# Convolved feed-forward, up projection: pairing high and low x in one 512-column matmul

## The chip, the cores and the metric

The kernel runs on one core of a Trainium2 chip. The metric is the device time of one execution in microseconds (us), the median of several runs. The engines are TensorE (PE; its weight loads are listed as PEld), VectorE (DVE), ScalarE (ACT), GpSimd (POOL) and SyncE (SP), which issues the weight stream's DMAs. Each engine works through its own list of instructions in order and waits only on semaphores.

## The reference

Two two-layer transformer blocks over 256 positions of width 1024, in float32. The part that is changed is the feed-forward of the second block, in both of its layers:

```python
h = rms_norm(x, norm_ffn_g[l])
u = causal_depthwise_conv(h @ ffn_w_up[l], ffn_conv_w[l], ffn_conv_b[l])   # 1024 -> 2 x 2816, 3 taps
x = x + (silu(u[..., :D_FF]) * u[..., D_FF:]) @ ffn_w_down[l]              # 2816 -> 1024
```

## The kernel before

**Numbers in two parts.** Every float32 operand of a product is split into a high part (rounded to fp32r) and a low part (the rest): a = ah + al. A product is three matmuls that add up in one PSUM bank: high weights with high x, high weights with low x, low weights with high x.

**The weight stream.** All weights come as units of 128 x 2048 numbers, in the order of use, through four slots (`raw`, `whi`, `wlo`). For unit U, SP loads `raw`; ScalarE makes the high part, `hi(U)` (L592), once the unit has landed and TensorE has used unit U - 4; VectorE makes the low part, `lo(U)` (L1143), and counts `lo_ready`, which frees `raw` for the next load and `whi`, `wlo` for TensorE. TensorE counts `unit_used`.

**The up product.** The 5632 columns are cut into CTF = 11 blocks, j = 0 to 10, of 512 columns: four groups f of 128, two of the gate half and two of the up half. A block takes two units, U1 + 2j and U1 + 2j + 1 (half the depth each). Block 0 is made with x as the stationary operand and turned; blocks 1 and 2 have the weights stationary and the x that isn't yet divided by its root mean square (`scaled_u` multiplies the result by the row `krow`); from j = RAW_X = 3 on the matmuls read `xs`, x already scaled: four rows of 1024, high m=0, low m=0, low m=1, high m=1, so that `xs_h` is rows 0 and 3 and `xs_l` rows 1 and 2. In `up_straight(j)` each group f and depth tile kt has three matmuls of 256 columns (L2518, L2520, L2521), 96 in a block. A block fills two PSUM banks; the eight banks (`acc` four, `tb` four) hold four blocks in turn (`up_bank`). The wait for block j is for the taps of block j - 4:

```python
elif j >= 4:
    pe.wait_ge(f_t2, CTF * l + j - 3)
```

**The convolution and gate.** For block j ScalarE makes `tap2(j)` (L1050, four instructions, tap 2 and the bias) from PSUM into `cv`; VectorE adds the other two taps, `taps10(j)` (L1710, eight instructions, from PSUM), and counts `f_t2`; ScalarE applies Silu, `fsilu(j)` (L1056); VectorE multiplies, `product(j)` (L1717, into `pr`); ScalarE makes the high part `fhi(j)` (L1063, into `yth`), VectorE the low part `flo(j)` (L1743, into `ytl`). Blocks 6 and 8 (`FSEVEN_POS`) go into a down product of seven instead of eight block products ("seven"); for it VectorE makes three sums, `y_sums` (L1727 to L1732), ScalarE their high part (L1067), VectorE their low part, `y_sums_lo` (L1738). In `fhi` ScalarE waits for these sums, and its copy for them follows.

**The order around it** is written out by hand. In the loop over j = 4 to 11 ScalarE has `hi(U1+2j+2)`, `tap2(j-1)`, `hi(U1+2j+3)`, `fsilu(j-2)`, `fhi(j-2)`, and VectorE `lo(U1+2j+2)`, `taps10(j-1)`, `lo(U1+2j+3)`, `product(j-2)`, `flo(j-2)`. The semaphores `f_t0`, `f_si`, `f_pr`, `f_hi` tie each step to the one of the other engine that it needs.

**The down product** (`out_product`) then takes 11 units with matmuls of 512 columns (L1850 to L1852), 24 for a plain unit. The sevens need the weights' sums (`sums`, L1153 to L1158, behind a `lo` of 1536 columns, L1141; ScalarE's `sums_hi`, L597; VectorE's `sums_lo`, L1163, into `fwsum_l`) before their fourth product.

Of the kernel before, what the change touches and what calls it, by code (L numbers as in the profile page):

```python
# [84 lines left out]
def two_blocks_kernel(nc, x_in, stream, cols, bs_col, ws_t, gs_row, fin_row, fin2_row, rel_rows, ffn_cw,  # L85
                      conv_w, conv_ln, moba_g, gla_g, gate_w, gate_b, gate_in, out):
    ctx = ExitStack()
    with ctx:
# [89 lines left out]
        fsum = at("fsum", [2 * 3 * P], o_sc)  # L178
        fsum_l = at("fsum_l", [2 * 3 * P], o_sc, F32R)
        fsum_h = at("fsum_h", [2 * 3 * P], o_sc + 2 * 3 * P, F32R)  # L180
        fwsum_at = (o_xh, o_sc + 5120)
        fwsum = [at(f"fwsum{i}", [2048], o) for i, o in enumerate(fwsum_at)]
        fwsum_l = [at(f"fwsum_l{i}", [2048], o, F32R) for i, o in enumerate(fwsum_at)]
        fwsum_h = [at(f"fwsum_h{i}", [2048], o + 2048, F32R) for i, o in enumerate(fwsum_at)]
# [51 lines left out]
        acc = [ctx.enter_context(nc.psum_tensor(f"acc{i}", [P, 512], F32)) for i in range(4)]  # L236
# [4 lines left out]
        def score_parts(b0, i):  # L241
# [17 lines left out]
        n_add, n_tr, n_gm, n_hi, n_lo, n_sq, n_ms, n_r = (  # L259
            sem("norm_" + n) for n in ("added", "transposed", "gained", "hi", "lo", "squared", "meaned", "rms"))  # L260
# [3 lines left out]
        side_made, x_r2 = sem("side_made"), sem("mix_own_rms")  # L264
        a_ev, a_vsq, a_vsum, a_ms, a_r, a_vn, a_sp, a_spc, a_y, y_banks, a_hi, a_lo = (
            sem("gmlp_" + n) for n in ("act", "v_squared", "v_summed", "v_meaned", "v_rms", "v_normed", "spatial",
# [12 lines left out]
        f_ev, f_tr, f_t0, f_t1, f_t2, f_si, f_pr, f_hi, f_lo = (  # L279
            sem("ffn_" + n) for n in ("kept", "transposed", "tap2", "tap1", "tap0", "silu", "product", "hi", "lo"))  # L280
# [3 lines left out]
        x_ltr, x_bn, x_ag, x_lms, x_lr, x_nrm, x_btr, x_sl = (  # L284
            sem("conv_ln_" + n) for n in ("transposed", "stats", "mean", "var", "rstd", "normed", "back", "silu"))
# [56 lines left out]


# [98 lines left out]
        def _(pool):  # L442
# [17 lines left out]

            def root(r, outer=None):

                pool.wait_ge(n_sq, 2 * r + 2)
                pool.tensor_scalar(ssq(r, 0, 2), ssq(r, 0, 2), 1.0 / D, EPS, ALU.mult, ALU.add).then_inc(n_ms, 1)
                pool.wait_ge(n_ms, r + 1)
                two = stat[:, 2 * r:2 * r + 2]
                last = pool.tensor_tensor(two, ssq(r, 0, 2), mhalf[:, 0:2], ALU.pow)
                if outer is not None:
                    last.then_inc(x_r2, 1)
                    pool.wait_ge(x_r2, 1)  # L470
                    last = pool.tensor_tensor(two, two, stat[:, 2 * outer:2 * outer + 2], ALU.mult)
                last.then_inc(n_r, 1)
# [31 lines left out]
            pool.tensor_scalar(stat[:, 66:68], stat[:, 64:66], 1.0 / DFF_A, EPS, ALU.mult, ALU.add).then_inc(a_ms, 1)  # L504
            pool.wait_ge(a_ms, 1)
# [26 lines left out]
            for l in range(2):  # L532
# [18 lines left out]
                pool.tensor_scalar(stat[:, 72:74], mvv[:, :, 1], 1.0, LN_EPS, ALU.mult, ALU.add).then_inc(x_lms, 1)  # L551
                pool.wait_ge(x_lms, l + 1)
# [23 lines left out]
        def _(act):  # L576
# [294 lines left out]
            for l in range(2):  # L871
# [222 lines left out]
                for j in range(4, CTF + 1):  # L1094
                    hi(U1 + 2 * j + 2)
                    tap2(j - 1)
                    hi(U1 + 2 * j + 3)
                    fsilu(j - 2)
                    fhi(j - 2)
                fsilu(CTF - 1)  # L1100
                fhi(CTF - 1)
                for j in range(4, CTF + 2):
                    if j == FSEVEN_POS[1] + 4:
                        first_sum(2 + l)
                    hi(U1 + 2 * CTF + j)
                    if j - 1 in FSEVEN_POS:
                        sums_hi(2 + l, FSEVEN_POS.index(j - 1))
# [25 lines left out]
        def _(dve):  # L1133
# [371 lines left out]
            for l in range(2):  # L1505
# [240 lines left out]
                def scaled_u(j):  # L1746
                    dve.wait_ge(unit_used, U1 + 2 * j + 2)
                    if j == 2:
                        dve.wait_ge(f_tr, l + 1)
                    else:  # L1750
                        dve.wait_ge(f_ev, 4 * l + 2)
                    row = krow[:, :].unsqueeze(1).to_broadcast([P, 2, SEQ])
                    for i in range(2):
                        o = dve.tensor_tensor(us[:, j % 2, i, :].rearrange("p (a t) -> p a t", t=SEQ),
                                              up_bank(j, pair, i)[:, :].rearrange("p (a t) -> p a t", t=SEQ), row, ALU.mult)
                    o.then_inc(f_ev, 1)
# [45 lines left out]
                for j in range(4, CTF + 2):  # L1802
# [45 lines left out]
        def _(pe):  # L1848
# [400 lines left out]
            for l in range(2):  # L2249
# [230 lines left out]
                def ffn_turn():  # L2480
                    pe.wait_ge(f_ev, 4 * l + 2)
# [16 lines left out]
                def up_straight(j):  # L2498
                    if j == 2:
                        pe.wait_ge(r_rc, l + 2)  # L2500
                    elif j == 3:
                        pe.wait_ge(f_ev, 4 * l + 2)
                        pe.wait_ge(x2_lo, 4 + 2 * l + 2)
                    elif j >= 4:
                        pe.wait_ge(f_t2, CTF * l + j - 3)
                    for half in range(2):
                        s = (U1 + 2 * j + half) % SLOTS
                        pe.wait_ge(lo_ready, U1 + 2 * j + half + 1)
                        for f in range(4):
                            o = up_bank(j, pair, f // 2)[:, SEQ * (f % 2):SEQ * (f % 2) + SEQ]  # L2510
                            if j >= RAW_X:
                                o = o.rearrange("p (m t) -> p m t", t=P)
                            for kk in range(4):
                                kt, ws = 4 * half + kk, slice(512 * kk + P * f, 512 * kk + P * f + P)
                                ks = slice(P * kt, P * kt + P)
                                xh = xth[:, kt, :] if j < RAW_X else xs_h[:, :, ks]
                                xl = xtl[:, kt, :] if j < RAW_X else xs_l[:, :, ks]
                                pe.matmul(o, whi[:, s, ws], xh, start=kt == 0 and f % 2 == 0, stop=False,  # L2518
                                          skip_group_check=True)
                                pe.matmul(o, whi[:, s, ws], xl, start=False, stop=False, skip_group_check=True)  # L2520
                                mm = pe.matmul(o, wlo[:, s, ws], xh, start=False, stop=kt == KT - 1,  # L2521
                                               skip_group_check=True)
# [7 lines left out]

                up_turned()
                for j in range(1, CTF):
                    up_straight(j)
# [99 lines left out]
```

## Time and profile before

| | |
|---|---|
| median of 3 runs | 1215.8 us (1215.56 to 1216.29) |
| profiled execution, its span | 1214.1 us; its own time is given by the span and what lies around it, 1.7 us if it ran at the median |
| busy | PE 1205.5, PEld 1048.0, DVE 903.9, ACT 671.1, POOL 51.3 us |
| DMA | 220.40 MB, mean 182 GB/s |

The span is the time from the first to the last instruction in the trace. Busy time is time with at least one instruction under way; matmuls overlap in the pipeline, so that TensorE's rate is read from the distance between starts and not from durations. The same holds for the other engines to a lesser degree: a group of one kind overlaps by some 0.08 us from one instruction to the next.

### The profile page before, as it was taken

Reading aid. Unit: us, or ns where it says so; the run is one execution under the profiler, and the core shown is the slowest. Engines: PE = TensorE matmul, PEld = TensorE weight load, DVE = VectorE, ACT = ScalarE, POOL = GpSimd, SP = SyncE. Lnnn points to the kernel's source line nnn. Section 1 sums busy time; section 2 is a strip of 40 time slices with the busy share of each in tenths; the row PEclk is TensorE's granted clock in tenths of the full one; section 3 lists DMA queues with packets and bytes.
Section 4 is the critical chain, followed back from the end, with each engine's and each line's share of the span. In section 5 each row is a group of like instructions: output and inputs, shape, how many; then the busy total and the mean of one; then the engine's idle time right before and its main releaser. Section 6 shows DMA issues by size and latency. Waiting matters only on the chain.

```text
span 1214.1 us, 17930 instructions
## 1 busy us (share of the span) xinstructions
PE 1205.5 (99%) x7099; PEld 1048.0 (86%) x7099; DVE 903.9 (74%) x1105; ACT 671.1 (55%) x807; POOL 51.3 (4%) x101
## 2 busy tenths in 40 slices
PE   9999999999999999999999999999999999999998
PEld 7888888888899888888888889999888888999986
DVE  5566465568886685566988986988887998698886
ACT  7655354445466664444648556555655755566553
POOL 2000000000010000000010020000001011000000
PEclk9999999999999999999999999999999999999999
DMA  9644645545654335554555454455574435555550
GB/s 349 232 164 168 223 147 200 194 163 196 243 191 166 131 141 206 207 179 168 193 214 174 139 177 161 152 205 174 174 262 161 140 107 184 191 179 180 196 196 35
DMA packets 32568, 220.40 MB, mean 182 GB/s; under 512 B 3888, under 2 KB 4048, under 8 KB 6768
## 3 DMA queue, kind: packets, MB, share of 16 engines
q1 hardware_dynamic: 29888, 212.33, 49.3%
q0 software_dynamic: 1664, 5.41, 1.3%
q10 hardware_dynamic: 944, 1.64, 0.4%
q8 instruction: 54, 0.88, 0.3%
q14 instruction: 18, 0.15, 0.0%
HBM read 218.31 MB, written 1.05 MB: 181 GB/s over the span
## 4 chain that ended last, share of the span: by engine, by line
PE 92%; DVE 6%; DMA 1%; issue 0%; POOL 0%; ACT 0%; ACTq 0%; POOLq 0%; DVEq 0%
PE acc L1850 20%; PE acc L1852 20%; PE acc L1851 20%; PE tb L1878 3%; PE tb L2521 3%; PE tb L2520 3%; PE acc L2520 3%; PE acc L2521 3%; PE tb L2518 3%; PE acc L2518 3%; DVE cacc L1534 3%; DVE wlo L1143 1%; PE acc L2158 1%; PE acc L2160 1%; PE acc L2161 1%; PE tb L1850 1%
## 5 line engine op out<-in xcount | busy, mean ns | idle before, releaser
L1143 DVE TENSOR_TENSOR wlo<-raw,whi 128x2048 fp32r<-128x2048 f32 x184 | 417.3, 2287 | 131.8 <-ACT whi L592 131.8
L592 ACT ACTIVATE whi<-raw 128x2048 fp32r<-128x2048 f32 (+1 forms) x198 | 368.4, 1882 | 56.5 <-PE acc L1852 43.9
L1850 PE MATMUL acc<-whi,xth 128*128 128x512 f32 x704 | 279.8, 397 | 0.6 <-DVE xtl L1241 0.5
L1852 PE MATMUL acc<-whi,xtl 128*128 128x512 f32 x704 | 274.7, 390 | 0.0
L1851 PE MATMUL acc<-wlo,xth 128*128 128x512 f32 x704 | 274.3, 390 | 0.0
L1850 PE MATMUL acc<-whi,yth 128*128 128x512 f32 (+1 forms) x428 | 169.0, 395 | 0.0
L1852 PE MATMUL acc<-whi,ytl 128*128 128x512 f32 (+1 forms) x428 | 166.6, 389 | 0.0
L1851 PE MATMUL acc<-wlo,yth 128*128 128x512 f32 (+1 forms) x428 | 166.4, 389 | 0.0
L1850 PEld LDWEIGHTS acc<-whi,xth 128*128 128x128 f32 x704 | 132.3, 188 | 28.0 <-DVE wlo L1232 1.3
L1852 PEld LDWEIGHTS acc<-whi,xtl 128*128 128x128 f32 x704 | 132.2, 188 | 28.1
L1851 PEld LDWEIGHTS acc<-wlo,xth 128*128 128x128 f32 x704 | 132.4, 188 | 25.7
L1852 PEld LDWEIGHTS acc<-whi,ytl 128*128 128x128 f32 x428 | 80.4, 188 | 16.8
L1850 PEld LDWEIGHTS acc<-whi,yth 128*128 128x128 f32 x428 | 80.4, 188 | 16.0 <-issue 0.5
L1851 PEld LDWEIGHTS acc<-wlo,yth 128*128 128x128 f32 x428 | 80.5, 188 | 15.6
L730 ACT ACTIVATE sg<-acc,stat 128x256 f32<-128x256 f32 x44 | 20.9, 475 | 93.9 <-PE acc L1852 93.9
L2521 PE MATMUL tb<-xs,wlo 128*128 128x256 f32 x256 | 72.5, 283 | 0.0
L2521 PE MATMUL acc<-xs,wlo 128*128 128x256 f32 x256 | 72.5, 283 | 0.0
L2518 PE MATMUL tb<-xs,whi 128*128 128x256 f32 x256 | 72.5, 283 | 0.0
L2520 PE MATMUL tb<-xs,whi 128*128 128x256 f32 x256 | 72.5, 283 | 0.0
L2520 PE MATMUL acc<-xs,whi 128*128 128x256 f32 x256 | 72.5, 283 | 0.0
L2518 PE MATMUL acc<-xs,whi 128*128 128x256 f32 x256 | 72.5, 283 | 0.0
L1340 DVE SCALAR_TENSOR_TENSOR yy<-acc,stat,sg 128x256 f32<-128x256 f32 x44 | 21.1, 480 | 63.1 <-ACT sg L730 63.1
(407 smaller groups left out, 1919.3 us busy)
## 6 DMA issues: line engine op xcount, KB each, us to landing
raw<-in_stream SPq DMA_DIRECT2D x200, 1024.0 KB, 5.0
rb<-in_rel_rows POOLq DMA_DIRECT2D x8, 256.0 KB, 2.9
x<-in_x_in ACTq DMA_DIRECT2D x4, 256.0 KB, 7.4
raw<-in_stream SPq DMA_DIRECT2D x2, 512.0 KB, 9.3
gs_sb<-in_gs_row POOLq DMA_DIRECT2D x1, 1024.0 KB, 7.6
frow<-in_fin_row POOLq DMA_DIRECT2D x2, 512.0 KB, 6.0
raw<-in_stream SPq DMA_DIRECT2D x2, 256.0 KB, 7.0
ws_sb<-in_ws_t POOLq DMA_DIRECT2D x1, 512.0 KB, 7.7
```

What stands on the lines that cost most here:

```text
L592: act.activation(whi[:, s, c0:UNIT], raw[:, s, c0:UNIT], ACT.Copy).then_inc(hi_ready, 1)
L730: act.activation(sg[:, j % 2, m, :], pair_bank(j + pair, m)[:, 0:256], ACT.Silu, scale=rms(STATS[k], m)).then_inc(g_silu, 1)
L1143: dve.tensor_tensor(wlo[:, s, :], raw[:, s, :], whi[:, s, :], ALU.subtract).then_inc(lo_ready, 1)
L1340: dve.scalar_tensor_tensor(yy[:, j % 2, m, :], pair_bank(j + pair, m)[:, 256:512], rms(STATS[k], m), sg[:, j % 2, m, :], ALU.mult, ALU.mul ...
L1534: dve.scalar_tensor_tensor(cacc[:, a, :], src, w, cacc[:, a, :], ALU.mult, ALU.add).then_inc(done, 1)
L1850: pe.matmul(o, xh, wh, start=first, stop=False)
L1851: pe.matmul(o, xh, wl, start=False, stop=False)
L1852: return pe.matmul(o, xl, wh, start=False, stop=last)
L1878: return pe.transpose(o, i, ident[0:n, 0:n])
L2518: pe.matmul(o, whi[:, s, ws], xh, start=kt == 0 and f % 2 == 0, stop=False, skip_group_check=True)
L2520: pe.matmul(o, whi[:, s, ws], xl, start=False, stop=False, skip_group_check=True)
L2521: mm = pe.matmul(o, wlo[:, s, ws], xh, start=False, stop=kt == KT - 1, skip_group_check=True)
```

## The change

From block 3 on, `up_paired(j)` takes the place of `up_straight(j)`. For each group f and depth tile, one matmul of 512 columns multiplies the high weights with all four rows of `xs`, and one of 256 columns multiplies the low weights with `xs_h` and adds to the outer two quarters of the bank. So a bank holds one group f: high product, low product, low product, high product. A block fills four banks, `accall` for odd j and `tball` for even j, and two blocks are in PSUM at once. ScalarE copies the low quarters into `us` (`low_kept`, two instructions), VectorE adds the high quarters to them in place (`joined`, two instructions) and counts `f_ev`; `tap2` and `taps10` of j >= 3 read `us` (in SBUF) instead of PSUM. The order of both engines' lists in the loop is new; the waits of TensorE and of the down product's first banks are for `joined` (`up_kept(l, j)` is the count). `fsum` and `fwsum` are at other places in SBUF, and GpSimd's own-step semaphores are merged into one.

```diff
-        fsum = at("fsum", [2 * 3 * P], o_sc)
+        fsum = at("fsum", [2 * 3 * P], o_xh)
...
+        accall = ctx.enter_context(nc.psum_tensor("acc", [P, 4, 512], F32))
+        acc = [accall[:, i, :] for i in range(4)]
...
+        def up_four(j):
+            return accall if j % 2 else tball
+
+        def up_kept(l, j):
+            return (CTF + 1) * l + 2 + j
...
-            if j in (1, 2):
+            if j:
                 return us[:, j % 2, a // 2, (a % 2) * SEQ:(a % 2 + 1) * SEQ]
...
+            def then_wait(op):
+
+                steps[0] += 1
+                op.then_inc(pool_step, 1)
+                pool.wait_ge(pool_step, steps[0])
...
+                def low_kept(j):
+                    act.wait_ge(f_t2, CTF * l + j - 1)
+                    act.wait_ge(unit_used, U1 + 2 * j + 2)
+                    for i in range(2):
+                        four = up_four(j)[:, 2 * i:2 * i + 2, :].rearrange("p f (b t) -> p f b t", t=P)
+                        o = act.activation(us[:, j % 2, i, :].rearrange("p (f m t) -> p f m t", f=2, t=P),
+                                           four[:, :, 1:3, :], ACT.Copy)
+                    o.then_inc(f_xl, 1)
+
                 def tap2(j):
                     if j == 0:
                         act.wait_ge(f_tr, l + 1)
-                    elif j < RAW_X:
-                        act.wait_ge(f_ev, 4 * l + 2 + j)
                     else:
-                        act.wait_ge(unit_used, U1 + 2 * j + 2)
+                        act.wait_ge(f_ev, up_kept(l, j))
...
-                for j in range(4, CTF + 1):
-                    hi(U1 + 2 * j + 2)
-                    tap2(j - 1)
-                    hi(U1 + 2 * j + 3)
-                    fsilu(j - 2)
-                    fhi(j - 2)
-                fsilu(CTF - 1)
-                fhi(CTF - 1)
-                for j in range(4, CTF + 2):
+                hi(U1 + 10)
+                fsilu(2)
+                fhi(2)
+                for j in range(RAW_X, CTF):
+                    low_kept(j)
+                    hi(U1 + 2 * j + 5)
+                    tap2(j)
+                    hi(U1 + 2 * j + 6)
+                    fsilu(j)
+                    fhi(j)
+                for j in range(5, CTF + 2):
...
+                def joined(j):
+                    dve.wait_ge(f_xl, (CTF - RAW_X) * l + j - RAW_X + 1)
+                    for i in range(2):
+                        four = up_four(j)[:, 2 * i:2 * i + 2, :].rearrange("p f (b t) -> p f b t", t=P)
+                        o = dve.tensor_tensor(us[:, j % 2, i, :].rearrange("p (f m t) -> p f m t", f=2, t=P),
+                                              four[:, :, 0:4:3, :],
+                                              us[:, j % 2, i, :].rearrange("p (f m t) -> p f m t", f=2, t=P), ALU.add)
                     o.then_inc(f_ev, 1)
...
-                for j in range(4, CTF + 1):
-                    lo(U1 + 2 * j + 2)
-                    taps10(j - 1)
-                    lo(U1 + 2 * j + 3)
-                    product(j - 2)
-                    if j - 2 in FSEVEN_POS:
-                        y_sums(j - 2)
-                    flo(j - 2)
-                    if j - 2 in FSEVEN_POS:
-                        y_sums_lo(j - 2)
-                product(CTF - 1)
+                lo(U1 + 10)
+                product(2)
+                for j in range(RAW_X, CTF):
+                    joined(j)
+                    flo(j - 1)
+                    if j - 1 in FSEVEN_POS:
+                        y_sums_lo(j - 1)
+                    lo(U1 + 2 * j + 5)
+                    taps10(j)
+                    lo(U1 + 2 * j + 6)
+                    product(j)
+                    if j in FSEVEN_POS:
+                        y_sums(j)
                 flo(CTF - 1)
...
+                def up_paired(j):
+                    if j == RAW_X:
+                        pe.wait_ge(f_ev, up_kept(l, 1))
+                        pe.wait_ge(x2_lo, 4 + 2 * l + 2)
+                    else:
+                        if j == RAW_X + 1:
+                            pe.wait_ge(f_t2, CTF * l + 1)
+                        pe.wait_ge(f_ev, up_kept(l, j - 2))
+                    for half in range(2):
+                        s = (U1 + 2 * j + half) % SLOTS
+                        pe.wait_ge(lo_ready, U1 + 2 * j + half + 1)
+                        for f in range(4):
+                            o = up_four(j)[:, f, :].rearrange("p (b t) -> p b t", t=P)
+                            for kk in range(4):
+                                kt, ws = 4 * half + kk, slice(512 * kk + P * f, 512 * kk + P * f + P)
+                                ks = slice(P * kt, P * kt + P)
+                                pe.matmul(o, whi[:, s, ws], xs[:, :, ks], start=kt == 0, stop=False, skip_group_check=True)
+                                mm = pe.matmul(o[:, 0:4:3, :], wlo[:, s, ws], xs_h[:, :, ks], start=False,
+                                               stop=kt == KT - 1, skip_group_check=True)
...
                     if isinstance(j, tuple):
-                        pe.wait_ge(f_t2, CTF * l + 10 - 2 * j[1])
+                        pe.wait_ge(f_ev, up_kept(l, CTF - 2))
```

## Rows read from the trace of the kernel before

**Rows 1.** The page: span, share of each engine, chain that ended last by engine.

```profile
span 1214.1 us, 17930 instructions
...
PE 1205.5 (99%) x7099; PEld 1048.0 (86%) x7099; DVE 903.9 (74%) x1105; ACT 671.1 (55%) x807; POOL 51.3 (4%) x101
...
PE 92%; DVE 6%; DMA 1%; issue 0%; POOL 0%; ACT 0%; ACTq 0%; POOLq 0%; DVEq 0%
```

**Rows 2.** Windows: first 20 us, blocks 3 to 10 of each layer.

```profile
core 0: us, PE busy (x) PEld busy (x) DVE busy (x) ACT busy (x) POOL busy (x), PEclk, DMA share, GB/s
0.00:20.00 20.00, 17.21 (x71) 13.11 (x72) 12.17 (x19) 12.69 (x19) 2.66 (x14) 1.00 0.88 332
767.90:860.06 92.16, 92.16 (x770) 92.16 (x769) 79.00 (x113) 55.22 (x69) 0.00 (x0) 1.00 0.53 183
1057.56:1149.72 92.16, 92.16 (x770) 92.16 (x769) 78.99 (x113) 55.22 (x69) 0.00 (x0) 1.00 0.54 183
```

**Rows 3.** Timeline of ACT (start, duration, instruction), two rounds of the loop.

```profile
804.72 0.63 ACT L1063 ACTIVATE yth<-pr 128x512 fp32r<-128x512 f32 x1 [4.28 <-DVE pr L1717]
805.26 1.90 ACT L592 ACTIVATE whi<-raw 128x2048 fp32r<-128x2048 f32 x1
...
839.26 1.90 ACT L592 ACTIVATE whi<-raw 128x2048 fp32r<-128x2048 f32 x1
```

**Rows 4.** Timeline of DVE, one round of the loop, then block 6.

```profile
804.00 0.68 DVE L1717 TENSOR_TENSOR pr<-cv 128x512 f32<-128x512 f32 x1
805.38 0.69 DVE L1743 TENSOR_TENSOR ytl<-pr,yth 128x512 fp32r<-128x512 f32 x1 [0.70 <-ACT yth L1063]
807.18 2.29 DVE L1143 TENSOR_TENSOR wlo<-raw,whi 128x2048 fp32r<-128x2048 f32 x1 [1.11 <-ACT whi L592]
809.39 3.33 DVE L1710 SCALAR_TENSOR_TENSOR cv<-acc,fcw,cv 128x255 f32<-128x255 f32 x8
812.64 2.28 DVE L1143 TENSOR_TENSOR wlo<-raw,whi 128x2048 fp32r<-128x2048 f32 x1
814.84 0.68 DVE L1717 TENSOR_TENSOR pr<-cv 128x512 f32<-128x512 f32 x1
...
836.53 0.68 DVE L1717 TENSOR_TENSOR pr<-cv 128x512 f32<-128x512 f32 x1
...
839.58 0.55 DVE L1738 TENSOR_TENSOR fsum_l<-fsum,fsum_h 128x384 fp32r<-128x384 f32 x1
```

**Rows 5.** Timeline of DVE, last steps before the loop.

```profile
782.23 3.36 DVE L1710 SCALAR_TENSOR_TENSOR cv<-us,fcw,cv 128x255 f32<-128x255 f32 x8
785.51 2.28 DVE L1143 TENSOR_TENSOR wlo<-raw,whi 128x2048 fp32r<-128x2048 f32 x1
```

**Rows 6.** Timeline of PE: down product's first matmul, then 16 matmuls' first and last.

```profile
860.06 0.40 PE L1850 MATMUL acc<-whi,yth 128*128 128x512 f32 x1
...
870.29 0.39 PE L1850 MATMUL acc<-whi,yth 128*128 128x512 f32 x1
...
873.69 0.39 PE L1850 MATMUL acc<-whi,yth 128*128 128x512 f32 x1
```

**Rows 7.** Timeline of ACT: evacuations of 512 elements from PSUM.

```profile
739.07 0.67 ACT L1036 ACTIVATE us<-acc,stat 128x512 f32<-128x512 f32 x1
...
953.51 0.60 ACT L936 ACTIVATE eG<-tb 128x512 f32<-128x512 f32 x1
954.00 0.59 ACT L937 ACTIVATE nG<-tb 128x512 f32<-128x512 f32 x1
```

**Rows 8.** Timeline of DVE: `scaled_u` and the instruction behind it.

```profile
775.42 1.28 DVE L1754 TENSOR_TENSOR us<-tb,krow 128x512 f32<-128x512 f32 x2
776.62 2.28 DVE L1143 TENSOR_TENSOR wlo<-raw,whi 128x2048 fp32r<-128x2048 f32 x1
```

**Rows 9.** Timeline of DVE in the down product: first seven.

```profile
881.62 1.75 DVE L1141 TENSOR_TENSOR wlo<-raw,whi 128x1536 fp32r<-128x1536 f32 x1
...
888.02 2.28 DVE L1163 TENSOR_TENSOR fwsum_l<-fwsum,fwsum_h 128x2048 fp32r<-128x2048 f32 x1
```

More of the change, by code:

```diff
@@ L177, in two_blocks_kernel @@
         usum = at("usum", [3, 512], o_sc)
-        fsum = at("fsum", [2 * 3 * P], o_sc)
[L179 to L184, printed above, removed]
+        fsum = at("fsum", [2 * 3 * P], o_xh)
+        fsum_l = at("fsum_l", [2 * 3 * P], o_xh, F32R)
+        fsum_h = at("fsum_h", [2 * 3 * P], o_xh + 2 * 3 * P, F32R)
+        fwsum_at = ((o_xh + 2048, o_sc), (o_sc + 5120, o_sc + 7168))
+        fwsum = [at(f"fwsum{i}", [2048], o) for i, (o, _) in enumerate(fwsum_at)]
+        fwsum_l = [at(f"fwsum_l{i}", [2048], o, F32R) for i, (o, _) in enumerate(fwsum_at)]
+        fwsum_h = [at(f"fwsum_h{i}", [2048], o, F32R) for i, (_, o) in enumerate(fwsum_at)]
         fusum = at("fusum", [3, 512], o_sc + 2048)
@@ L258, in two_blocks_kernel @@
             sem(n) for n in ("consts_loaded", "consts_made", "made"))
-        n_add, n_tr, n_gm, n_hi, n_lo, n_sq, n_ms, n_r = (
-            sem("norm_" + n) for n in ("added", "transposed", "gained", "hi", "lo", "squared", "meaned", "rms"))
+        n_add, n_tr, n_gm, n_hi, n_lo, n_sq, n_r = (
+            sem("norm_" + n) for n in ("added", "transposed", "gained", "hi", "lo", "squared", "rms"))
         x2_z, x2_hi, x2_lo = sem("second_x_scaled"), sem("second_x_hi"), sem("second_x_lo")
@@ L278, in two_blocks_kernel @@
         w_hi, w_lo = (sem("attn_out_" + n) for n in ("hi", "lo"))
-        f_ev, f_tr, f_t0, f_t1, f_t2, f_si, f_pr, f_hi, f_lo = (
-            sem("ffn_" + n) for n in ("kept", "transposed", "tap2", "tap1", "tap0", "silu", "product", "hi", "lo"))
+        f_xl, f_ev, f_tr, f_t0, f_t1, f_t2, f_si, f_pr, f_hi, f_lo = (
+            sem("ffn_" + n) for n in ("low_x_kept", "kept", "transposed", "tap2", "tap1", "tap0", "silu", "product", "hi", "lo"))
         x_ld, x_gh, x_gl, x_g16 = sem("gate_loaded"), sem("gate_hi"), sem("gate_lo"), sem("gate_kept")
@@ L283, in two_blocks_kernel @@
             sem("conv_" + n) for n in ("padded", "sigmoid", "gated", "transposed", "kept", "tap"))
-        x_ltr, x_bn, x_ag, x_lms, x_lr, x_nrm, x_btr, x_sl = (
-            sem("conv_ln_" + n) for n in ("transposed", "stats", "mean", "var", "rstd", "normed", "back", "silu"))
+        x_ltr, x_bn, x_ag, x_lr, x_nrm, x_btr, x_sl = (
+            sem("conv_ln_" + n) for n in ("transposed", "stats", "mean", "rstd", "normed", "back", "silu"))
         x_ev = sem("mix_kept")
@@ L459, in _ @@
                                pattern=[[-GCH, P // GCH], [0, GCH]], channel_multiplier=1).then_inc(consts_made, 1)
+            steps = [0]
+            def then_wait(op):
+                steps[0] += 1
+                op.then_inc(pool_step, 1)
+                pool.wait_ge(pool_step, steps[0])
             def root(r, outer=None):
                 pool.wait_ge(n_sq, 2 * r + 2)
-                pool.tensor_scalar(ssq(r, 0, 2), ssq(r, 0, 2), 1.0 / D, EPS, ALU.mult, ALU.add).then_inc(n_ms, 1)
-                pool.wait_ge(n_ms, r + 1)
+                then_wait(pool.tensor_scalar(ssq(r, 0, 2), ssq(r, 0, 2), 1.0 / D, EPS, ALU.mult, ALU.add))
                 two = stat[:, 2 * r:2 * r + 2]
@@ L468, in root @@
                 if outer is not None:
-                    last.then_inc(x_r2, 1)
-                    pool.wait_ge(x_r2, 1)
+                    then_wait(last)
                     last = pool.tensor_tensor(two, two, stat[:, 2 * outer:2 * outer + 2], ALU.mult)
@@ L1789, in _ @@
                 taps10(2)
[L1790 to L1800 removed]
+                lo(U1 + 10)
[11 more added lines that the diff above has]
+                        y_sums(j)
                 flo(CTF - 1)
[L1802 removed]
+                for j in range(5, CTF + 2):
                     lo(U1 + 2 * CTF + j)
@@ L2480, in ffn_turn @@
                 def ffn_turn():
[L2481 removed]
+                    pe.wait_ge(f_ev, up_kept(l, 0))
                     for a in range(4):
@@ L2510, in up_straight @@
                             o = up_bank(j, pair, f // 2)[:, SEQ * (f % 2):SEQ * (f % 2) + SEQ]
-                            if j >= RAW_X:
-                                o = o.rearrange("p (m t) -> p m t", t=P)
                             for kk in range(4):
                                 kt, ws = 4 * half + kk, slice(512 * kk + P * f, 512 * kk + P * f + P)
[L2515 to L2518, printed above, removed]
+                                pe.matmul(o, whi[:, s, ws], xth[:, kt, :], start=kt == 0 and f % 2 == 0, stop=False,
                                           skip_group_check=True)
-                                pe.matmul(o, whi[:, s, ws], xl, start=False, stop=False, skip_group_check=True)
-                                mm = pe.matmul(o, wlo[:, s, ws], xh, start=False, stop=kt == KT - 1,
+                                pe.matmul(o, whi[:, s, ws], xtl[:, kt, :], start=False, stop=False, skip_group_check=True)
+                                mm = pe.matmul(o, wlo[:, s, ws], xth[:, kt, :], start=False, stop=kt == KT - 1,
                                                skip_group_check=True)
```

29 lines of the change are left out of this document (13 added, 16 removed).

## Prediction

> **What bounds the kernel now.** I read the head of the page first: TensorE (PE) is busy for 99% of the span, the chain that ended last is 92% PE, and the granted clock is 1.00, its upper level of 2.4 GHz, in the windows [rows 1, 2]. Read alone, that says that a shorter TensorE stream is a shorter kernel. So the second view is the windows over the stretch that the change rewrites: blocks j = 3 to 10 of the up product, one stretch in each layer. Each is 92.16 us = 8 x 11.52 us; TensorE is busy throughout, VectorE (DVE) for 79.0 us, ScalarE (ACT) for 55.2 us [rows 2]. VectorE is at 86%, so the third view must be the order of events on the other two engines.
>
> That timeline shows a second bound just under the first. From one `product` to the next is 814.84 - 804.00 = 10.84 us [rows 4], and both engines wait on each other inside it: `product` (VectorE) releases `fhi` (ScalarE), which releases `flo`; ScalarE's next `hi` releases VectorE's next `lo`, and VectorE stands idle 0.70 and 1.11 us at those two places. My sum of one round from the rows gives the same: 0.54 (`fhi`) + 1.93 (`hi`, until `lo` starts) + 2.21 (`lo`) + 3.25 (`taps10`) + 2.20 (`lo`) + 0.71 (`product`, until `fhi` starts) = 10.84 [rows 3, 4]. TensorE needs 11.52 us per block, so today this loop gains 0.68 us a block and hides. It hides though it starts late: block 3 ends at 767.90 + 11.52 = 779.4, but `taps10(2)` runs until 785.5 [rows 2, 5]. That lateness is allowed because TensorE waits, at block j, only for the taps of j - 4.
>
> **The change, part by part.** *TensorE.* Starts of 256-column matmuls lie 92.16 / 768 = 0.120 us apart [rows 2]; 15 steps of 512-column ones take 873.69 - 870.29 = 3.40 us, so 0.2267 each [rows 6]. A pair (256 high x, 256 low x) becomes one of 512: 0.240 to 0.2267, 13.3 ns saved. There are 2 layers x 8 blocks x 32 = 512 such pairs, so 6.8 us if TensorE stays the bound. A block is then 32 x (0.2267 + 0.120) = 11.09 us. The columns are unchanged; I take the strided 256-column write of the low-weight matmul at 0.120, as xs is already read in strides at that pace.
>
> The Trainium skill, "TensorE: Matmul & The Clock Gate", section "Back-to-back issue gap", gives an isolated warm gap of N/2.4 + 2.5 ns. By it (an estimate from that page) a removed matmul would be worth 2.5 ns and the whole gain 1.3 us; the rows show 13.3 ns here.
>
> *ScalarE, `low_kept`.* Two copies of 512 elements from PSUM per block, 32 in all. Nearest row: a 512-element evacuation takes 0.60 us and the next starts 0.49 later [rows 7]; I take 0.50, so 0.50 + 0.60 + 0.03 for the hand-over = 1.13 us until `joined` can start. With a scale operand one took 0.67 [rows 7]; that bounds it above at about 1.29. Below: no cheaper row of this size, so 1.10.
>
> *VectorE, `joined`.* Two additions of 512 elements, one operand in PSUM. The pair of `scaled_u` has that shape: 1.28 us to the end of the pair, 1.20 until the next instruction starts [rows 8]; with the small wait I take 1.22. Bounds 1.18 and 1.28.
>
> *Taps.* They now read the copy in SBUF: `taps10` 3.28 us from SBUF (782.23 to 785.51) against 3.25 from PSUM (809.39 to 812.64) [rows 4, 5]. `tap2` lengthens slightly on ScalarE, which has room and isn't on the loop there.
>
> *The loop's order.* Block j's round is now, on the path: `joined(j)` 1.22, `flo(j-1)` 0.61, `lo` 2.20, `taps10(j)` 3.28, `lo` 2.20, `product(j)` 0.71, then on ScalarE `fhi(j)` 0.54 and `low_kept(j+1)` 1.13. Sum 11.89 us. `hi(U1+2j+5)` comes behind `low_kept(j)` and ends about when `flo` does (1.00 + 1.91 + 0.03 = 2.94 against 2.96), so it costs nothing; with `flo` earlier it would. The old idle time of 1.81 us (0.70 + 1.11) is replaced by about as much: VectorE idles through `fhi` and `low_kept`. Hence the loop grows by roughly `joined` less what little overlap is rearranged, from 10.84 to 11.89, above both 11.09 and the old 11.52.
>
> *The new wait.* A block fills four PSUM banks, so TensorE may start block j only when `joined(j-2)` is done. Slack: `joined(j-2)` has one block, 11.09 us, behind the end of j-2. Behind that waiting matmul is TensorE's whole queue.
>
> *Where the loop starts.* Up to `taps10(2)` both programs are the same. The freed VectorE then runs `lo(U1+10)` 785.51 to 787.71 [rows 5] and `product(2)`; `fhi(2)` starts at 787.71 + 0.68 + 0.03 = 788.42, `low_kept(3)` at 788.96, `joined(3)` at 790.09 and ends at 791.37. Block 3 starts at 767.90, so TensorE is ready for block 5 at 767.90 + 2 x 11.09 = 790.08: it waits 1.3 us at once and from there runs at the loop's pace. The product may start when `joined(9)` is done, six rounds on. Blocks 6 and 8 are the "seven" ones: their `y_sums` and the extra copy put 839.26 - 836.53 = 2.73 us between `product` and the next ScalarE step, where a plain block has 805.26 - 804.00 = 1.26, so 1.47 more [rows 3, 4]; the round after each has `y_sums_lo`, 0.55 us long, so 0.47 more until the next start [rows 4]. Rounds: three of 11.89, then 13.36, 12.36, 13.36 = 74.75 us. `joined(9)` ends at 791.37 + 74.75 = 866.12; the down product starts at 866.15 where it starts at 860.06 today [rows 6]: 6.1 us later.
>
> *Does the down product give anything back?* No: TensorE is packed there (0.2267 pace) and its length doesn't depend on the delay. Does it add? TensorE reaches the wait for `fwsum_l` in the first seven (unit 6) after (6 x 24 + 9) x 0.2267 = 34.7 us. VectorE's road there from the end of `joined(9)`: 12.30 until `joined(10)` gives it free, then 0.61, 2.20, 3.28, 2.20 (`flo`, `lo`, `taps10`, `lo`), 0.71, 0.54, 1.93 (`product`, `fhi`, `hi`), 2.20 (`lo`), 6.40 for the seven's `lo` and `sums` and the next `lo` (888.02 - 881.62), and 2.28 for `fwsum_l` itself [rows 9]: 34.65. That just fits, where today it ends at 890.30 and is wanted at 860.06 + 34.68 = 894.7, 4.4 us to spare; I add nothing to the value and up to 1 us a layer to the range.
>
> *Edits at no cost:* POOL's own-step semaphores are merged with the same waits in the same order, and POOL has nothing in these stretches [rows 2]; fsum and fwsum move address; weight loads fall with the matmuls they overlap. The refills of raw by SP wait for `lo`, which comes later, but each slot is refilled a round ahead of its use.
>
> *Sum.* The second layer repeats the first to 0.01 us in these windows [rows 2], so 2 x 6.1 = 12.2. Span 1214.1 + 12.2 = 1226.3; the median of the runs, 1215.8, lies 1.7 over the span, so 1228.0 us.
>
> **The rivals.** *A: TensorE remains the bound.* Then 6.8 us are gained: 1209.0 us. It decides if the loop's round is under 11.09 us and `joined(3)` ends before 790.08, 1.3 us sooner than I have it. For it: 99% busy PE. Against: the sum of today's round, by the same method, hits 10.84, and `joined` alone is added to it. Chance 0.07. If only part of it holds (a round near 11.4), the two effects cancel: within 0.2%, 0.02.
>
> *B: the loop is longer than I have it.* Each 0.1 us in `low_kept` or `joined` counts seven times a layer, 1.4 us in all; strided banks at 0.15 us more for each of the four instructions would give 8.4 us and stalls at the tight seven: about 1238. No row shows these shapes; for it speaks that `low_kept` and `joined` step over two banks at once, against it that `tap2` and `taps10` read the same banks at the pace of the SBUF copy. Chance 0.06.
>
> *C: the clock falls in the new gaps.* TensorE will pause about once a block, for 0.8 to 2.3 us. In the first 20 us it stood idle 2.8 us in sum, and the clock shows 1.00 [rows 2]. If the level of 1.2 GHz were granted for a quarter of each 11 us block, TensorE would need some 13.9 us a block and set the pace: (13.9 - 11.9) x 14 = 28 us more, 1256. Chance 0.03. The skill's same page, in "Why this matters for your kernels", warns of longer gaps than these; no gap of that kind stands in this trace.
>
> **Chances and range.** My forecast, a loop of 11.8 to 12.1 us, has 0.82 and gives 1226.5 to 1232. The bounds (1.10 to 1.29, 1.18 to 1.28) move each round by -0.07 to +0.22, so -1.0 to +3.1 us in all, with up to 2 us from the down products. I widen to 1224.5 to 1234 for what the hand-overs may hide. A change under 0.2% (2.4 us) is about what this measurement can't tell from none. Faster 0.07, same 0.02, slower 0.91.
>
> **What would show it.** Right: the first TensorE idle time in each layer before block 5's first 512-column matmul, released by VectorE's `joined`; starts of `joined` 11.9 us apart, 13.4 around blocks 6 and 8; TensorE idle near 9.6 us a layer; 512-column matmuls 0.227 apart; the down product 6.1 us later than today. Wrong: no idle TensorE in the stretch (rival A), a 512-element `low_kept` or `joined` well over 0.7 us (B), a PEclk under 1.00 (C), or a pause that `lo` ends instead of `joined`, which would mean I have mis-ordered the loop.

## The result, and the profile after

The changed kernel takes 1230.2 us (median of 4 runs, 1227.3 to 1231.2) against 1215.9: a ratio of 1.0114, 95% interval 1.0100 to 1.0128. It is 14.3 us slower; 12.2 us were forecast.

The head of the page answers to [rows 1]: 512 matmuls fewer, and a chain that is no longer TensorE alone.

```profile
span 1229.5 us, 16986 instructions
...
PE 1208.1 (98%) x6587; PEld 1022.4 (83%) x6587; DVE 922.0 (75%) x1137; ACT 690.8 (56%) x839; POOL 51.3 (4%) x101
...
PE 74%; DVE 22%; ACT 2%; issue 1%; DMA 1%; POOL 0%; ACTq 0%; POOLq 0%; DVEq 0%
```

TensorE's share of the chain falls from 92 to 74%, VectorE's rises from 6 to 22%. The windows over the same stretches as in [rows 2], block 3's first matmul to the down product's, then the first 5 us behind each:

```profile
core 0: us, PE busy (x) PEld busy (x) DVE busy (x) ACT busy (x) POOL busy (x), PEclk, DMA share, GB/s
768.00:866.10 98.10, 91.58 (x514) 78.07 (x513) 83.18 (x123) 62.63 (x81) 0.00 (x0) 1.00 0.50 172
1065.29:1163.37 98.08, 91.37 (x515) 77.93 (x513) 83.17 (x123) 62.63 (x81) 0.00 (x0) 1.00 0.49 172
866.00:871.00 5.00, 4.90 (x15) 3.92 (x16) 4.96 (x8) 4.19 (x6) 0.00 (x0) 0.66 0.18 25
1163.00:1168.00 5.00, 4.63 (x14) 3.69 (x14) 5.00 (x8) 4.45 (x6) 0.00 (x0) 0.66 0.16 23
```

There are two things to see. Each stretch is 98.1 us instead of 92.16, so 5.9 us longer, and TensorE is busy for only some 91.5 us of it. And behind each stretch the mean granted clock is 0.66: 0.34 x 5 = 1.7 us lost, twice. The sum is 5.94 + 5.92 + 1.7 + 1.7 = 15.3 us; the spans differ by 1229.5 - 1214.1 = 15.4. The waits name what TensorE waited for (us in total, times, and the longest in us):

```profile
PE acc L2568 <- DVE us L1782: 5.7, 6, 1.7
PE acc L1881 <- DVE us L1782: 3.9, 2, 2.0
PE tb L2568 <- DVE us L1782: 3.6, 6, 0.9
```

L1782 is `joined`. All fourteen pauses end with it: six blocks and the down product, in each layer. VectorE's timeline, first steps and a plain round (it answers to [rows 4, 5]):

```profile
785.62 2.29 DVE L1163 TENSOR_TENSOR wlo<-raw,whi 128x2048 fp32r<-128x2048 f32 x1
787.82 0.69 DVE L1737 TENSOR_TENSOR pr<-cv 128x512 f32<-128x512 f32 x1
790.18 1.29 DVE L1782 TENSOR_TENSOR us<-acc,us 128x512 f32<-128x512 f32 x2 [1.67 <-ACT us L1055]
791.39 0.68 DVE L1763 TENSOR_TENSOR ytl<-pr,yth 128x512 fp32r<-128x512 f32 x1
791.99 2.29 DVE L1163 TENSOR_TENSOR wlo<-raw,whi 128x2048 fp32r<-128x2048 f32 x1
794.19 3.36 DVE L1730 SCALAR_TENSOR_TENSOR cv<-us,fcw,cv 128x255 f32<-128x255 f32 x8
797.47 2.29 DVE L1163 TENSOR_TENSOR wlo<-raw,whi 128x2048 fp32r<-128x2048 f32 x1
799.67 0.69 DVE L1737 TENSOR_TENSOR pr<-cv 128x512 f32<-128x512 f32 x1
802.03 1.29 DVE L1782 TENSOR_TENSOR us<-tb,us 128x512 f32<-128x512 f32 x2 [1.67 <-ACT us L1055]
...
864.67 1.29 DVE L1782 TENSOR_TENSOR us<-acc,us 128x512 f32<-128x512 f32 x2 [2.08 <-ACT us L1055]
```

`joined` starts at 790.18 and 802.03, 11.85 us apart, and for block 9 at 864.67. Ahead of it, in the plain rounds (those without the sums for blocks 6 and 8), VectorE is idle for 1.67 us, while ScalarE does `fhi` and `low_kept`:

```profile
788.54 0.63 ACT L1081 ACTIVATE yth<-pr 128x512 fp32r<-128x512 f32 x1 [2.17 <-DVE pr L1737]
789.08 1.07 ACT L1055 ACTIVATE us<-acc 128x512 f32<-128x512 f32 x2
790.03 1.91 ACT L603 ACTIVATE whi<-raw 128x2048 fp32r<-128x2048 f32 x1
```

The two copies of `low_kept` take 1.07 us, 0.95 until the next instruction starts. At the end of the stretch, TensorE's timeline shows the pause and, a little later, the slower clock:

```profile
863.74 0.40 PE L2568 MATMUL tb<-xs,whi 128*128 128x512 f32 x1
863.97 0.28 PE L2569 MATMUL tb<-xs,wlo 128*128 128x256 f32 x1
866.10 0.47 PE L1881 MATMUL acc<-whi,yth 128*128 128x512 f32 x1 [1.85 <-DVE us L1782]
866.41 0.39 PE L1882 MATMUL acc<-wlo,yth 128*128 128x512 f32 x1
...
867.09 0.63 PE L1882 MATMUL acc<-wlo,yth 128*128 128x512 f32 x1
867.52 0.63 PE L1883 MATMUL acc<-whi,ytl 128*128 128x512 f32 x1
867.94 0.63 PE L1881 MATMUL acc<-whi,yth 128*128 128x512 f32 x1
```

From 867.09 on, 512-column matmuls start 0.43 us apart instead of 0.227: the granted clock is at its lower level, 1.2 GHz.

### The profile page after: what moved, and what is told of

Read it like the earlier page. It is cut to its first block, busy times and chain, and to the rows that moved or that the text cites. A ratio compares the mean times of both kernels' runs of the same rounds, so it can differ in the third digit from the quotient of the medians.

```text
span 1229.5 us, 16986 instructions
## 1 busy us (share of the span) xinstructions
PE 1208.1 (98%) x6587; PEld 1022.4 (83%) x6587; DVE 922.0 (75%) x1137; ACT 690.8 (56%) x839; POOL 51.3 (4%) x101
## 4 chain that ended last, share of the span: by engine, by line
PE 74%; DVE 22%; ACT 2%; issue 1%; DMA 1%; POOL 0%; ACTq 0%; POOLq 0%; DVEq 0%
PE acc L1881 20%; PE acc L1883 20%; PE acc L1882 20%; DVE wlo L1163 8%; DVE cv L1730 5%; PE tb L1909 3%; DVE cacc L1554 3%; DVE us L1782 1%; PE acc L2189 1%; PE acc L2191 1%; PE acc L2192 1%; ACT us L1055 1%; DVE pr L1737 1%; PE tb L1882 1%; PE tb L1883 1%
## 5 line engine op out<-in xcount | busy, mean ns | idle before, releaser
L2568 PE MATMUL acc<-xs,whi 128*128 128x512 f32 x256 | 90.4, 398 | 5.7 <-DVE us L1782 5.7
L2568 PE MATMUL tb<-xs,whi 128*128 128x512 f32 x256 | 91.0, 400 | 3.6 <-DVE us L1782 3.6
L1730 DVE SCALAR_TENSOR_TENSOR cv<-us,fcw,cv 128x255 f32<-128x255 f32 (+1 forms) x160 | 66.6, 478 | 3.3 <-ACT cv L1068 2.6
L2568 PEld LDWEIGHTS acc<-xs,whi 128*128 128x128 f32 x256 | 48.0, 188 | 18.7 <-DVE us L1782 7.6
```

What stands on the lines that cost most here:

```text
L1730: o = dve.scalar_tensor_tensor(dst, src, fcw[:, l, c:c + 1], dst, ALU.mult, ALU.add)
L2568: pe.matmul(o, whi[:, s, ws], xs[:, :, ks], start=kt == 0, stop=False, skip_group_check=True)
```

## The experiments

Theory: the chain through ScalarE and VectorE, 11.85 us a block, sets TensorE's pace, since block j waits for `joined(j-2)`. Rivals: TensorE's own stream counts; VectorE's added work is what costs, in whatever order; the shallower depth in PSUM costs. All runs are compared with the kernel before on the same chip, 1215.8 to 1216.0 us.

### TensorE's matmuls taken apart again

```diff
-                                pe.matmul(o, whi[:, s, ws], xs[:, :, ks], start=kt == 0, stop=False, skip_group_check=True)
+                                pe.matmul(o[:, 0:4:3, :], whi[:, s, ws], xs_h[:, :, ks], start=kt == 0, stop=False,
+                                          skip_group_check=True)
+                                pe.matmul(o[:, 1:3, :], whi[:, s, ws], xs_l[:, :, ks], start=False, stop=kt == KT - 1,
+                                          skip_group_check=True)
```

> The changed kernel with the 512-column matmul taken apart again into two of 256 columns (high x, low x) into the same four banks; all else as changed. A block on TensorE is again 11.52 us instead of 11.09. My theory (the ScalarE-VectorE loop of 11.85 us a block sets the pace): no loss from it, joined(9) ends where it did, span without clock loss 1225.6 to 1226.5, median 1227 to 1231 as the changed kernel; TensorE's pauses become 0.43 us shorter, so the one before the down product shrinks from 2.1 to 1.7 us and, if pauses of 2 us are what costs the clock, PEclk stays 1.00 more often. Rival (TensorE still counts for the end): 6.8 us slower, about 1236.

Measured: 1227.8 us (1227.5 to 1227.9), ratio 1.0098 (1.0083 to 1.0114). With 512 more matmuls the kernel is no slower than the changed one, and all four runs lie beside the changed kernel's fastest (1227.3). That the median is 2.4 us lower goes with the clock: this trace has no fall behind its two stretches. The windows:

```profile
core 0: us, PE busy (x) PEld busy (x) DVE busy (x) ACT busy (x) POOL busy (x), PEclk, DMA share, GB/s
767.84:865.92 98.08, 93.87 (x771) 92.48 (x769) 83.16 (x123) 62.62 (x81) 0.00 (x0) 1.00 0.51 172
1063.54:1161.64 98.10, 93.84 (x771) 92.45 (x769) 83.19 (x123) 62.62 (x81) 0.00 (x0) 1.00 0.50 172
```

The same 98.1 us with 2.3 us more busy time in TensorE. So TensorE's stream doesn't count in the changed kernel, and the first rival falls.

### One more copy on ScalarE

```diff
+        spare = const("spare", [2 * P])
...
                     act.wait_ge(unit_used, U1 + 2 * j + 2)
+                    act.activation(spare[:, :], up_four(j)[:, 0, P:3 * P], ACT.Copy)
                     for i in range(2):
```

> The changed kernel with one more ScalarE copy of 256 elements from PSUM into a spare tile ahead of low_kept's two; its result is used by nobody. My theory: it lies on the loop, 0.28 us in each of 7 rounds a layer, so starts of joined go from 11.85 to 12.13 us apart and the time grows by 14 x 0.28 = 3.9 us (plus 1.7 us for each further fall of the clock). Rival (joined's place on VectorE, 86 to 92 per cent busy, is the bound, not the chain through both engines): ScalarE has room, so no change.

Measured: 1233.9 us (1232.0 to 1234.8), ratio 1.0145 (1.0129 to 1.0161), 3.7 us over the changed kernel. The clock falls in runs of both, so the medians alone would not settle 3.9 us. `joined` (here L1784) now starts 12.12 us apart, 0.27 more, and VectorE's idle time ahead of it grows by 0.28:

```profile
803.08 1.29 DVE L1784 TENSOR_TENSOR us<-tb,us 128x512 f32<-128x512 f32 x2 [1.95 <-ACT us L1057]
...
815.20 1.29 DVE L1784 TENSOR_TENSOR us<-acc,us 128x512 f32<-128x512 f32 x2 [1.95 <-ACT us L1057]
```

The two stretches settle it:

```profile
core 0: us, PE busy (x) PEld busy (x) DVE busy (x) ACT busy (x) POOL busy (x), PEclk, DMA share, GB/s
768.52:868.53 100.01, 93.24 (x514) 79.58 (x513) 83.17 (x123) 64.52 (x88) 0.00 (x0) 0.98 0.49 169
1066.30:1166.31 100.01, 92.88 (x515) 79.42 (x513) 83.17 (x123) 64.53 (x88) 0.00 (x0) 0.98 0.49 169
```

Each is 100.01 us, 1.91 and 1.93 more than in the changed kernel: seven times 0.27. ScalarE is busy for 56% of the span, and yet 0.27 us of work on it costs 14 x 0.27 = 3.8 us. What counts is the chain, not either engine's share. The clock fell three times in this trace, and two of the falls lie inside the stretches (behind the pause before block 9: PEclk 0.98 over the whole stretch, 0.66 over the 5 us from 842.2). They cost nothing: both stretches are as long as the loop alone makes them, because TensorE would have waited there anyway.

### The order alone

```diff
-                fhi(2)
                 for j in range(RAW_X, CTF):
                     low_kept(j)
+                    fhi(j - 1)
                     hi(U1 + 2 * j + 5)
                     tap2(j)
                     hi(U1 + 2 * j + 6)
                     fsilu(j)
-                    fhi(j)
+                fhi(CTF - 1)
```

> The changed kernel with ScalarE's order altered: low_kept(j) stands ahead of fhi(j-1), so that joined(j) finds its operand when product(j-1) is done. No work is added or taken away. My theory: VectorE's 1.67 us pause before joined goes; the round is then set by fhi and hi before the next lo: from product 0.71 + 0.54 + 1.93 (until lo starts) + 2.20 + 3.28 + 2.20 = 10.86 us, below TensorE's 11.09. joined(9) ends about 1.2 us after TensorE needs it (the seven rounds take 12.3), so 2.2 us per layer faster than before the change: 1211.5 us, range 1210 to 1213, PEclk 1.00 or one fall. Rival (VectorE's added 1.2 us of joined is what costs, whatever the order): still 1228 or more.

Measured: 1212.2 us (1212.1 to 1212.6), ratio 0.9971 (0.9960 to 0.9982): the same instructions, another order on one engine, and the loss of 14.3 us is a gain of 3.6. On VectorE `joined` follows `product` directly, and the only idle time left is ahead of `lo`:

```profile
798.17 0.68 DVE L1737 TENSOR_TENSOR pr<-cv 128x512 f32<-128x512 f32 x1
798.77 1.28 DVE L1782 TENSOR_TENSOR us<-tb,us 128x512 f32<-128x512 f32 x2
799.97 0.68 DVE L1763 TENSOR_TENSOR ytl<-pr,yth 128x512 fp32r<-128x512 f32 x1
801.36 2.29 DVE L1163 TENSOR_TENSOR wlo<-raw,whi 128x2048 fp32r<-128x2048 f32 x1 [0.71 <-ACT whi L603]
803.57 3.36 DVE L1730 SCALAR_TENSOR_TENSOR cv<-us,fcw,cv 128x255 f32<-128x255 f32 x8
806.85 2.28 DVE L1163 TENSOR_TENSOR wlo<-raw,whi 128x2048 fp32r<-128x2048 f32 x1
809.05 0.68 DVE L1737 TENSOR_TENSOR pr<-cv 128x512 f32<-128x512 f32 x1
809.65 1.28 DVE L1782 TENSOR_TENSOR us<-acc,us 128x512 f32<-128x512 f32 x2
```

The round is 809.65 - 798.77 = 10.88 us (10.86 expected). `joined` still takes its 1.28 us, so VectorE's added work isn't what costs. The second rival falls. The time came within the forecast by another sum than mine, though: I had TensorE's stretch at 88.7 us and a pause of about 1.2 us at its end, and the trace has no pause there and a stretch of 90.45 us (767.48 to 857.93, TensorE busy throughout). The next run shows why.

### The next copy, and high weights, ahead of `fhi`

```diff
-                fhi(2)
                 for j in range(RAW_X, CTF):
                     low_kept(j)
                     hi(U1 + 2 * j + 5)
+                    fhi(j - 1)
                     tap2(j)
                     hi(U1 + 2 * j + 6)
                     fsilu(j)
-                    fhi(j)
+                fhi(CTF - 1)
```

> As the run before, but hi(U1+2j+5) too stands ahead of fhi(j-1). My theory: flo and lo both find their operands, VectorE's round is its own work, 10.1 us (11.2 and 10.6 with the sevens' sums), TensorE never waits: a block at 11.09 us, each layer's stretch 88.7 instead of 92.16 us, no pause in TensorE, PEclk 1.00, 1215.9 - 6.8 = 1209.1 us, range 1208.5 to 1211. Rival (the pairing itself saves nothing, its pace is the columns'): 1215.8. Rival (VectorE's work is the limit): over 1215.8.

Measured: 1212.5 us (1211.8 to 1212.6), ratio 0.9972 (0.9961 to 0.9983). VectorE's round became 10.17 us, and TensorE doesn't pause in the stretch, but the time is 3.4 us above the forecast of 1209.1 and outside its range (1208.5 to 1211). The windows show where:

```profile
767.98:858.43 90.45, 90.45 (x514) 78.40 (x513) 88.02 (x130) 67.04 (x86) 0.00 (x0) 1.00 0.55 188
1056.00:1146.46 90.46, 90.46 (x515) 78.50 (x513) 88.02 (x130) 67.06 (x86) 0.00 (x0) 1.00 0.55 188
```

A stretch is 90.45 us and all of it busy TensorE, so a block takes 11.31 us and not 11.09. The starts:

```profile
793.07 0.40 PE L2568 MATMUL acc<-xs,whi 128*128 128x512 f32 x1
793.31 0.28 PE L2569 MATMUL acc<-xs,wlo 128*128 128x256 f32 x1
793.42 0.40 PE L2568 MATMUL acc<-xs,whi 128*128 128x512 f32 x1
...
794.48 0.40 PE L2568 MATMUL acc<-xs,whi 128*128 128x512 f32 x1
```

Four pairs take 794.48 - 793.07 = 1.41 us, 0.353 each. I had forecast 0.2267 + 0.120 = 0.347. That halves the pairing's gain: 0.360 - 0.353 = 7 ns, not 13.3, for each of 512 pairs, 3.4 us. It also explains why this order gives nothing over the last: TensorE is the bound in both, with the same 90.45 us. The next three runs ask for the reason; each keeps ScalarE's order of this one.

### Four and four instead of in turn

```diff
                             for kk in range(4):
                                 ...
                                 pe.matmul(o, whi[:, s, ws], xs[:, :, ks], start=kt == 0, stop=False, skip_group_check=True)
+                            for kk in range(4):
                                 ...
                                 mm = pe.matmul(o[:, 0:4:3, :], wlo[:, s, ws], xs_h[:, :, ks], start=False,
```

> The reordered kernel of the last run (e4), with TensorE's order altered inside each group f: four 512-column matmuls, then the four of 256 columns, instead of one of each in turn. There, pairs in turn lay 0.3534 us apart, not 0.2267 + 0.120 = 0.3467. Theory 1 (the turn between lengths costs, about 7 ns per change from one to the other and back): a quarter of the changes, so 0.0017 us per pair are left, a block is 11.15 us and the time 1212.4 - 16 x 0.16 = 1209.8 us. Theory 2 (the 512-column matmul itself is slower here, 0.233 to 0.241, because it reads four strided rows of xs): the starts stay at 0.233 or more for all of them, no gain, 1212.4 us. Theory 3 (the strided write of the 256-column matmul): no gain either.

Measured: 1211.2 us (1211.0 to 1211.3), ratio 0.9961 (0.9947 to 0.9975). The stretch is 89.8 us, 0.66 us shorter:

```profile
core 0: us, PE busy (x) PEld busy (x) DVE busy (x) ACT busy (x) POOL busy (x), PEclk, DMA share, GB/s
767.94:857.73 89.79, 89.79 (x514) 78.48 (x513) 87.39 (x129) 67.02 (x86) 0.00 (x0) 1.00 0.55 189
```

### Sixteen and sixteen

The two loops over kk become two loops over f and kk, so that a half block has its sixteen long matmuls first.

```diff
                         for f in range(4):
                             o = up_four(j)[:, f, :].rearrange("p (b t) -> p b t", t=P)
                             for kk in range(4):
                                 ...
                                 pe.matmul(o, whi[:, s, ws], xs[:, :, ks], start=kt == 0, stop=False, skip_group_check=True)
+                        for f in range(4):
+                            o = up_four(j)[:, f, :].rearrange("p (b t) -> p b t", t=P)
+                            for kk in range(4):
                                 ...
                                 mm = pe.matmul(o[:, 0:4:3, :], wlo[:, s, ws], xs_h[:, :, ks], start=False,
```

> As e5_grouped, but over a whole half block: sixteen 512-column matmuls over the four banks, then sixteen of 256 columns. Theory 1: a sixteenth of the changes, 11.10 us a block, 1209.1 us. Theories 2 and 3: 1212.4 us. If changing the bank between matmuls costs, it is slower than e5_grouped, since the banks come round twice as often.

Measured: 1209.7 us (1209.4 to 1209.8), ratio 0.9949 (0.9934 to 0.9964): the fastest version, 6.3 us below the kernel before. The windows:

```profile
767.75:856.89 89.14, 89.14 (x514) 78.78 (x513) 86.74 (x127) 67.00 (x86) 0.00 (x0) 1.00 0.54 189
1054.41:1143.59 89.18, 89.18 (x514) 78.79 (x513) 86.78 (x127) 67.02 (x86) 0.00 (x0) 1.00 0.54 189
```

89.15 us, 11.14 a block. In turn 11.31, four and four 11.22, sixteen and sixteen 11.14: fewer changes of length, less time. The middle value was forecast lower (11.15), so the cost isn't strictly one amount per change. The starts also answer the second theory, that a 512-column matmul is slower because it reads four strided rows of `xs`:

```profile
790.09 3.82 PE L2568 MATMUL acc<-xs,whi 128*128 128x512 f32 x16
793.75 2.08 PE L2574 MATMUL acc<-xs,wlo 128*128 128x256 f32 x16
```

Sixteen of them take 793.75 - 790.09 = 3.66 us, 0.229 each, near the 0.2267 of the down product, and the theory wanted 0.233 or more.

### The low-weight product into the inner quarters

```diff
-                                mm = pe.matmul(o[:, 0:4:3, :], wlo[:, s, ws], xs_h[:, :, ks], start=False,
+                                mm = pe.matmul(o[:, 1:3, :], wlo[:, s, ws], xs_h[:, :, ks], start=False,
```

> The reordered kernel (e4) with the low-weight product added to the inner two quarters of the bank, which lie side by side, instead of the outer two; joined adds the quarters up, so the sum is the same. Theory 3 (the strided write costs the 7 ns): pairs at 0.3467, a block 11.09, 1209.0 us. Theories 1 and 2: pairs stay at 0.3534, 1212.4 us.

Measured: 1212.5 us (1211.8 to 1214.2), ratio 0.9973 (0.9963 to 0.9983), as with the outer quarters, and the stretch is 90.45 us in both traces. The strided write costs nothing.

### The kernel before, two blocks deep

```diff
-                    elif j >= 4:
+                    elif j == 4:
                         pe.wait_ge(f_t2, CTF * l + j - 3)
+                    elif j >= 5:
+                        pe.wait_ge(f_t2, CTF * l + j - 1)
```

> The kernel before, where TensorE waits for the taps of block j - 2 instead of j - 4 from block 5 on, as deep as the changed kernel's banks allow; nothing else. My theory (the shallower wait alone is harmless, it hurts only with the longer loop): taps10(3) ends at 791.0, 0.1 us behind TensorE's end of block 4, then the 10.84 us loop runs ahead of 11.52 us blocks; with the sevens' 12.3 us round once 0.1 to 0.5 us more; 0.1 to 1 us slower than before in all, 1215.9 to 1216.9. Rival (the depth is what costs the changed kernel its time): 1225 or more.

Measured: 1216.6 us (1216.2 to 1216.8), ratio 1.0005 (0.9996 to 1.0014). The shallower depth alone costs at most some 0.6 us, within what was forecast; the interval also allows none. The trace shows where it would come from: one delay of some 0.3 us in each layer, at the first matmul of block 5, and none behind it. So the third rival falls, as the reason by itself: two blocks of depth matter in the changed kernel because the loop behind them is longer than a block.

### Grouped matmuls in the order of the change

The matmuls of the sixteen-and-sixteen version, with ScalarE's order as the change has it.

> The changed kernel with TensorE's matmuls grouped as in e6 (a block 11.13 instead of 11.31 us) but ScalarE's order left as the change has it. My theory (the 11.85 us loop sets the pace): TensorE's gain only lengthens its pauses by 0.18 us, joined(9) ends where it did, span 1225.6 us plus 1.7 us for each fall of the clock; with pauses of about 2.2 and 2.3 us, longer than the changed kernel's, falls in every run, two or more: median 1229 to 1233. Rival for the clock (falls come by chance, not with the pauses' length): as often as in the changed kernel, 1227 to 1231. Rival (TensorE's pace counts): 2.6 us faster than the changed kernel.

Measured: 1229.4 us (1229.1 to 1230.7), ratio 1.0113 (1.0096 to 1.0130). TensorE's quicker stream again gives nothing: both stretches are 98.1 us, as in the changed kernel. What I forecast of the clock, at least two falls in every run, was wrong. The profiled run has one, behind the last pause (mean clock 0.66 from 1161.5 to 1166.5, 1.00 from 865.8 to 870.8); the three others took 1229.1, 1229.3 and 1230.7 us.

## Why the prediction was right

*The loop.* Forecast as 11.89 us from eight rows of before, it measured 11.85. Most of the difference is `low_kept`: `joined` starts 1.10 us after it (790.18 - 789.08), where I took 1.13. `joined` is 1.29 us, forecast 1.28. The first `joined` started at 790.18 (forecast 790.09), `joined(9)` ended at 864.67 + 1.29 = 865.96 (forecast 866.12), and the down product began at 866.10 (forecast 866.15). That the loop and nothing else sets the pace is shown by three interventions: TensorE's work up, no change; ScalarE's work on the chain up, the time up by fourteen times that; the order altered, the loss gone.

*The old waits.* That "the loop grows by roughly `joined`" was right in size, but the experiments put the cause more sharply. It is `fhi` and `low_kept` standing in a row between `product` and `joined`; out of that row, `joined` fits into VectorE's time.

*The down product.* Forecast to give nothing back and to need no more time. In the windows the two stretches and the two falls of the clock account for 15.3 of 15.4 us, so that was right. The first seven was less tight than I had it. In the run with the matmuls taken apart, where no fall delays TensorE, `fwsum_l` is done at 900.38 and first used at 900.91, so 0.5 us are to spare where I found 0.05. Part of this is a misreading: today's first use is at 895.00, not 894.7.

*The clock, rival C.* I held it apart from the forecast with 0.03, at 28 us for a quarter of each block. It came beside the forecast and not instead of it, and far smaller: in the profiled run two falls of 1.7 us, behind the pauses before the down products, none behind the six others of each layer. What follows the stretch confirms the size: from the down product's start to the end of the span the second layer takes 1229.5 - 1163.37 = 66.1 us, and 1226.1 - 1161.64 = 64.5 in the run with the matmuls taken apart, which has no fall there. A PEclk under 1.00 was my own sign that the forecast is wrong; it appeared, and my sum has no term for it. The runs' spans, 1229.5, 1229.4, 1227.6 and 1225.6 us, lie apart by 1.8 and 2.0 us: two, two, one and no fall would give this; only the first has its trace here. These falls are why the median passed the forecast, by 2.2 us. That it still lies in the range is in part luck: the upper end was put at 1234 for longer copies and for the down products, which needed none of it, and not for the clock. The forecast without a fall, 1228.0, stands beside the 1227.3 us of the fastest run and the 1227.8 us of the run with TensorE's matmuls taken apart, whose pauses are shorter and whose trace has no fall.

The Trainium skill, "TensorE: Matmul & The Clock Gate", section "Why this matters for your kernels", warns of pauses longer than any in this stretch. By this trace pauses of some 2 us between starts (863.97 to 866.10) were already followed by the lower level. What decides between a pause that is followed by a fall and one that isn't is open, and its length alone doesn't: TensorE was idle for 1.85 us before a fall here and for 1.98 us without one in the last experiment, where three of four such pauses had none.

*A term that was mis-sized without effect.* The pair of matmuls: 0.347 us forecast, 0.353 measured. In the changed kernel TensorE waits anyway, so it cost the forecast nothing. In rival A it would have: 6.8 us of gain were not to be had in this order of matmuls, only 3.4; with sixteen and sixteen they become 2 x (92.16 - 89.16) = 6.0. The step that failed was to add two paces that were each measured in a uniform stream. It also shows in a sign that missed: I had TensorE idle near 9.6 us a layer, and the window has 98.10 - 91.58 = 6.5. Slower pairs fill 8 x 0.22 = 1.8 us of that, and the rest is for the most part that the profile counts a pause from the modelled end of the last matmul (0.28 us after its start) and not from where the next could have started (0.12).

## What to carry to other kernels

Before trusting a bound of 99% busy, add up the round of the loop that feeds it: which instruction releases which across the engines. Here that round was 10.84 us behind a block of 11.52, so whatever is put onto the chain beyond 0.68 us a block is paid for in time (beyond 0.47 once the paired block takes 11.31). And a copy that releases an addition belongs ahead of work that no one waits for yet. With short and long matmuls in one stream, run them in groups; here the paces of uniform streams came close to adding up only then (0.348 us a pair against 0.347).

## What was not expected of the hardware

A 512-column and a 256-column matmul in turn take 0.353 us a pair, against 0.2267 + 0.120 in uniform streams and 11.14 / 32 = 0.348 when sixteen of each follow one another. The strided write isn't the cause (1212.5 us with and without it), and neither are the four strided rows that the long matmul reads (0.229 us each in a row of sixteen). What is left is the change from one length to the other; why it costs is open.

The granted clock fell after TensorE had paused for 2.1 us between starts, in a stream that was otherwise dense, and each fall behind a stretch cost some 1.7 us (a mean clock of 0.66 over 5 us). In the traces here TensorE had been idle for 1.85 to 2.23 us before each such fall, while idle times of up to 1.98 us passed without one. A fall inside a stretch in which TensorE waits for the loop anyway cost nothing: two stretches of 100.01 us with one each.
